# The last tile rows of a mixture-of-experts block: their weighting, adding and norm spread over ScalarE, GpSimd and TensorE

## The chip, the cores and the metric

The kernel runs on one core of a Trainium2 chip, in one launch. Its time is device microseconds of an execution. Three executions of the kernel before took 1188.94, 1193.68 and 1197.59 us, so the median is 1193.68 us. The profile is of a fourth execution, of 1189.59 us, in which the instructions span 1187.8 us.

## The reference

The program computes one transformer block on 512 tokens of width 1024 in f32: a token mixer of two branches, then a mixture of 32 experts of which each token takes two, then a norm. The change touches the end of it alone:

```python
    # hier_moe: each token has two entries (token, expert, weight), sorted by expert
    hid = jax.nn.silu(xblk @ w_gate[e]) * (xblk @ w_up[e])
    yb = hid @ w_down[e]
    y = segment_sum(yb * buf_w[:, None], buf_tok, num_segments=N + 1)[:N]
    ...
    h = h + gt2 * y
    return rmsnorm(h, norm_final_g)
```

`rmsnorm` divides each row of h by the root of its mean square plus 1e-6 and multiplies it with the gain of the final norm.

## The kernel before, in words

**Staging.** The experts are worked in 16 pairs (NPAIR). A pair has 128 rows, 64 for each expert. Per pair, TensorE multiplies the gathered tokens with the gate and up weights (L2638), ScalarE applies the silu (L2189), VectorE the product (L2393), TensorE transposes (L2648) and multiplies with the down weights in two halves of 512 columns (L2661), and VectorE multiplies each half with the gate row of the block into `yo` (`finish`, L2402). Rows of all pairs but the last are stored by GpSimd with an indirect DMA in `y_dram` at the two places of each token (`store`, L2116). The rows of the last pair never go to memory: `matrix(15)` holds, for each of the four tiles of 128 tokens, a 128x128 matrix with the weight of each entry at its token, and TensorE multiplies `yo` with it.

**The four tiles.** The 512 tokens lie in four tiles, i = 0 to 3 (the first to the fourth), and `h[:, i, :]` is tile i, 128x1024 f32. At the end SP loads for each tile two blocks of rows from `y_dram`, j = 0 and 1, 512 KB each (L2071): `ya[2*i]` lies in `uT` and `ya[2*i+1]` in `mg`. Each load has a semaphore `f_in` of its own. `wts[:, j, i]` is a token's weight for its entry j.

**The steps for a tile**, and who does them before the change:
- `summed(i)` (L2438, VectorE, tiles 0 to 2): two instructions of the form h = ya * weight + h, 128x1024 each, with both large inputs in SBUF.
- TensorE's sum (L2737): for tiles 0 to 2 the matrix of the last pair times `yo`. Tile 3 has no `summed`: two diagonal matrices (`diag`, in `wr`) times the loaded rows are added in the same PSUM banks, ahead of the matrix term. It counts `f_c`.
- `whole(i)` (L2482, VectorE): h = h + PSUM. It counts `f_h`.
- ScalarE's square with a sum along the row (L2220), then the root (L2222). The square's output goes to a PSUM bank as `junk`. It counts `f_rt`.
- `normed(i)` (L2486 and L2487, VectorE): reciprocal, then h * reciprocal * gain into `ya[2*i]`, again with two SBUF inputs. It counts `f_o`, and SP stores the tile (L2090).

**What sets the order.** Every engine has a queue written out by hand; an engine stops at each of its waits, and what is queued behind stands still. Chains (`f_link`, `link`) make an engine wait for its own last instruction. `further` (L2005) is a branch that every engine passes just before the end; its body, for tokens beyond the 16 pairs, isn't entered in the profiled execution. ScalarE's functions lie in tables, and a table is loaded by an instruction of its own wherever the one needed may not be there.

Of the kernel before, what the change touches and what calls it, by code (L numbers as in the profile page):

```python
# [150 lines left out]
def build(nc, A, out):  # L151
# [14 lines left out]
    with ExitStack() as top:  # L166
        stage_sems = []

        def sem(name):
            stage_sems.append(nc.alloc_semaphore(name))  # L170
            return stage_sems[-1]
# [1822 lines left out]
        def matrix(b):  # L1994

            return zrT[:, 2 + b % 2, :].rearrange("p (i t) -> p i t", i=NT)
# [1 line left out]
        diag = wr[:, :, :].rearrange("p k n -> p (k n)")[:, 0:2 * P].rearrange("p (j t) -> p j t", j=2)  # L1998
        yo_over = zrT[:, 6:8, :].rearrange("p a n -> p (a n)")
        mat_over = zrT[:, 0, :].rearrange("p (i t) -> p i t", i=NT)  # L2000
        bank_of = (0, 4, 6, 2)

        def two_banks(i):
            return ps[:, bank_of[i]:bank_of[i] + 2, :].rearrange("p b n -> p (b n)")
# [13 lines left out]
        ya = [(uT, mg)[j][:, :, :].rearrange("p a b -> p (a b)")[:, D * i:D * i + D] for i in range(NT) for j in range(2)]  # L2018
        f_in = [sem(f"f_in{n}") for n in range(2 * NT)]
        f_ld, f_warm, f_eps, f_h, f_sq, f_rt, f_o, f_out, f_dve = (sem(f"f_{n}") for n in "ld warm eps h sq rt o out dve".split())  # L2020
        out_t = out[0].rearrange("(i p) d -> i p d", p=P)

        with nc.Block() as block:
            @block.sync
            def _(sp):
# [39 lines left out]
                for q_ in range(2):  # L2065
                    sp.wait_ge(y_st[q_], 16 * (NPAIR // 2 - q_))
                    s_, turns = place_of("g", NPAIR - 1, q_)
                    sp.wait_ge(unit_free[s_], turns + 1 + fills[s_])
                for i in range(NT):
                    for j in range(2):  # L2070
                        sp.dma_start(ya[2 * i + j], y_rows[i, j]).then_inc(f_in[2 * i + j], 16)  # L2071

# [13 lines left out]
                sp.wait_ge(m_h0, 16)  # L2086
                sp.wait_ge(f_ld, 16)
                for i in range(NT):
                    sp.wait_ge(f_o, i + 1)
                    sp.dma_start(out_t[i], ya[2 * i]).then_inc(f_out, 16)  # L2090
                sp.wait_ge(f_out, 16 * NT)

            @block.gpsimd
            def _(pool):
                pool.memset(eps[:, :], 1e-6).then_inc(f_eps, 1)
                pool.wait_ge(m_yTe, NT)
                pool.dma_start(grow2, A["norm_ffn_g"][0].partition_broadcast(P)).then_inc(m_g, 16)
                pool.wait_ge(m_p, 8)
                pool.memset(xg, 0.0).then_inc(x_clear, 1)
                for i in range(NT):  # L2100
                    pool.wait_ge(n2_u, i + 1)
                    pool.dma_start(u2_dram[P * i:P * i + P, :], u2[:, i % 2, :]).then_inc(n2_row, 16)
                    pool.wait_ge(n2_row, 16 * (i + 1))
                pool.wait_ge(m_g, 16)

                def gather(b):
                    q_ = b % 2
                    wait(pool, e_xT, b - 1)
                    pool.indirect_dma_start(xg[:, q_, :], None, u2_dram,
                                            bass.IndirectOffsetOnAxis(ap=slots[:, b:b + 1], axis=0),  # L2110
                                            bounds_check=T - 1, oob_is_err=False)\
                        .then_inc(x_in[q_], 16)

                def store(b):
                    pool.wait_ge(e_y, 2 * b + 2)
                    pool.indirect_dma_start(y_dram, bass.IndirectOffsetOnAxis(ap=y_at[:, b:b + 1], axis=0), yo[:, b % 2, :],  # L2116
                                            None, bounds_check=2 * T - 1, oob_is_err=False)\
                        .then_inc(y_st[b % 2], 16)

                pool.wait_ge(r_sl, 1)  # L2120
                pool.wait_ge(x_clear, 1)
                gather(0)
                gather(1)
                pool.wait_ge(r_ya, 1)
                for b in range(NPAIR):
                    if b + 2 < NPAIR:
                        gather(b + 2)
                    if b < NPAIR - 1:
                        store(b)
                for q_ in range(2):  # L2130
                    pool.wait_ge(y_st[q_], 16 * (NPAIR // 2 - q_))

                def first():
                    pool.wait_ge(e_xT, NPAIR)
                    pool.wait_ge(e_wat, 1)

                def body(v):
                    pool.tensor_copy(idx[:, 0:1], slots[:, bass.ds(v + NPAIR, 1)]).then_inc(v_idx, 1)
                    pool.tensor_copy(ovw[:, 0:1], tok_at[:, bass.ds(v + NPAIR, 1)]).then_inc(v_tok, 1)
                    pool.tensor_copy(ovw[:, 1:2], w_at[:, bass.ds(v + NPAIR, 1)]).then_inc(v_wt, 1)  # L2140
                    pool.wait_ge(v_idx, v + 1)
                    pool.sem_inc(v_seen, 1)
                    pool.indirect_dma_start(xg[:, 0, :], None, u2_dram,
                                            bass.IndirectOffsetOnAxis(ap=idx[:, 0:1], axis=0),
                                            bounds_check=T - 1, oob_is_err=False).then_inc(v_x, 16)
                    pool.wait_ge(v_c, NT * v + NT)
                    pool.sem_inc(v_seen, 1)

                further(pool, first, body)

            @block.scalar
            def _(act):
# [58 lines left out]

                further(act, first, body)

                junk = ps[:, 0:2, :].rearrange("p b n -> p (b n)")
                act.wait_ge(f_warm, 1)
                for i in range(NT):
                    act.wait_ge(f_h, i + 1)
# [8 lines left out]
            def _(dve):  # L2226
# [253 lines left out]
                def whole(i):  # L2480
                    dve.wait_ge(f_c, i + 1)
                    dve.tensor_tensor(h[:, i, :], h[:, i, :], two_banks(i), ALU.add).then_inc(f_h, 1)  # L2482

                def normed(i):
                    dve.wait_ge(f_rt, i + 1)
                    f_link(dve.reciprocal(frt[:, i:i + 1], frt[:, i:i + 1]))  # L2486
                    dve.scalar_tensor_tensor(ya[2 * i], h[:, i, :], frt[:, i:i + 1], gf, ALU.mult, ALU.mult)\  # L2487
                        .then_inc(f_o, 1)

                summed(1)  # L2490
                whole(0)
                summed(2)
                whole(1)
                for i in range(2, NT):
                    normed(i - 2)
                    whole(i)
                normed(NT - 2)
                normed(NT - 1)

            @block.tensor  # L2500
            def _(pe):
# [220 lines left out]
                    pe.wait_ge(v_c, NT * OVER)  # L2722

                further(pe, first, body, last)
                pe.wait_ge(e_y, 2 * NPAIR)
                pe.wait_ge(e_mat, 1)
                for i in range(NT):
                    if i == NT - 1:
                        pe.wait_ge(e_diag, 2)
                        for j in range(2):  # L2730
                            pe.wait_ge(f_in[2 * i + j], 16)
                    for c in range(2):
                        cols = slice(512 * c, 512 * c + 512)
                        terms = [(diag[:, j, :], ya[2 * i + j][:, cols]) for j in range(2)] if i == NT - 1 else []
                        terms.append((matrix(NPAIR - 1)[:, i, :], yo[:, (NPAIR - 1) % 2, cols]))
                        for m, (one, rows) in enumerate(terms):
                            ins = pe.matmul(ps[:, bank_of[i] + c, :], one, rows, start=(m == 0), stop=(m == len(terms) - 1))  # L2737
                    ins.then_inc(f_c, 1)


# [26 lines left out]
```

## Time and profile before

| what | value |
|---|---|
| three executions | 1188.94, 1193.68, 1197.59 us |
| the profiled execution | 1189.59 us |
| its span | 1187.8 us |
| TensorE busy | 1032.5 us (87%) |
| VectorE busy | 418.4 us (35%) |
| ScalarE busy | 204.0 us (17%) |
| GpSimd busy | 150.4 us (13%) |
| last instruction of VectorE ends | 1184.8 us into the span |

The busy shares are means over the whole span. The change touches the last 25 us, where the shares are others: TensorE's last product ends near 1178.7 us, and VectorE is busy nearly without a gap from 1164.4 us on. What that stretch costs is read there, instruction by instruction.

### The profile page before, as it was taken

Reading aid. Unit: us, or ns where it says so; the run is one execution under the profiler, and the core shown is the slowest. Engines: PE = TensorE matmul, PEld = TensorE weight load, DVE = VectorE, ACT = ScalarE, POOL = GpSimd, SP = SyncE. Lnnn points to the kernel's source line nnn. Section 1 sums busy time; section 2 is a strip of 40 time slices with the busy share of each in tenths; the row PEclk is TensorE's granted clock in tenths of the full one; section 3 lists DMA queues with packets and bytes.
Section 4 is the critical chain, followed back from the end, with each engine's and each line's share of the span. In section 5 each row is a group of like instructions: output and inputs, shape, how many; then the busy total and the mean of one; then the engine's idle time right before and its main releaser. Section 6 shows DMA issues by size and latency. Waiting matters only on the chain.

```text
span 1187.8 us, 13390 instructions
## 1 busy us (share of the span) xinstructions
PE 1032.5 (87%) x5421; PEld 503.8 (42%) x5421; DVE 418.4 (35%) x736; ACT 204.0 (17%) x441; POOL 150.4 (13%) x219
## 2 busy tenths in 40 slices
PE   5999999999999898998999668988777788878775
PEld 4443344455445565766455423333333233333332
DVE  4663436563072653457424531111111111110016
ACT  4011123332102564222111100000000000000003
POOL 4100001141200544212000010000000000000000
PEclk9899999999998899999999869999999998998998
DMA  9923427323946001000971569999999999999995
GB/s 351 384 92 106 175 73 283 123 74 148 248 117 163 14 1 37 29 2 2 370 291 52 236 232 431 425 427 427 427 428 426 427 426 428 427 425 428 405 387 216
DMA packets 75760, 301.81 MB, mean 254 GB/s; under 512 B 21478, under 2 KB 27976, under 8 KB 63409
## 3 DMA queue, kind: packets, MB, share of 16 engines
q1 hardware_dynamic: 62178, 280.11, 59.8%
q0 software_dynamic: 6912, 15.59, 3.5%
q10 hardware_dynamic: 6608, 5.24, 1.5%
q8 instruction: 44, 0.72, 0.2%
q14 instruction: 18, 0.15, 0.0%
HBM read 286.03 MB, written 22.03 MB: 259 GB/s over the span
## 4 chain that ended last, share of the span: by engine, by line
PE 25%; DMA 21%; DVE 3%; issue 2%; ACT 1%; DVEq 0%; ACTq 0%; POOLq 0%
PE ps L2638 11%; DMA ring<-in_moe_w_down_dram 9%; DMA ring<-in_moe_w_gate_dram 8%; PE ps L2661 5%; PE ps L2579 5%; PE ps L2530 3%; DMA uT<-in_moe_w_gate_dram 3%; DMA uT<-y_dram 1%; DMA y_dram<-zrT,y_at 1%; PE ps L2546 1%; PE ps L2621 1%; DVE zrT L2385 1%; DVE h L2438 0%; DMA zrT<-u_dram,slots 0%; DVE uT L2487 0%
## 5 line engine op out<-in xcount | busy, mean ns | idle before, releaser
L2638 PE MATMUL ps<-ring,zrT 128*64 128x512 f32 x704 | 204.6, 631 | 40.9 <-issue 17.5
L1047 PE MATMUL ps<-ring,uT 128*128 128x512 f32 x384 | 169.8, 596 | 0.6 <-PE ps L965 0.6
L2638 PEld LDWEIGHTS ps<-ring,zrT 128*64 128x64 f32 x704 | 69.0, 145 | 141.0 <-issue 141.0
L1036 PE MATMUL ps<-uT,ring 128*128 128x512 f32 x256 | 117.3, 615 | 2.0 <-DVE uT L701 1.4
L2402 DVE TENSOR_TENSOR zrT<-ps,mod 128x512 f32<-128x512 f32 x32 | 22.1, 692 | 266.6 <-PE ps L2661 266.3
L1047 PEld LDWEIGHTS ps<-ring,uT 128*128 128x128 f32 x384 | 71.4, 190 | 86.5 <-issue 86.0
L2661 PE MATMUL ps<-ring,hdT 128*64 128x512 f32 x352 | 79.6, 604 | 18.7 <-DMA ring<-in_moe_w_down_dram 16.0
L2189 ACT ACTIVATE zrT<-ps 128x512 f32<-128x512 f32 x16 | 9.6, 597 | 413.4 <-PE ps L2638 413.4
L2638 PE MATMUL ps<-uT,zrT 128*64 128x512 f32 x160 | 72.3, 606 | 6.5 <-issue 6.5
L1036 PEld LDWEIGHTS ps<-uT,ring 128*128 128x128 f32 x256 | 49.4, 197 | 66.7 <-issue 65.4
L2116 POOL DMA_INDIRECT y_dram<-zrT,y_at x15 | 15.2, 1015 | 418.6 <-DVE zrT L2402 418.6
L2393 DVE TENSOR_TENSOR zrT<-zrT,ps 128x512 f32<-128x512 f32 x16 | 11.0, 688 | 143.4 <-PE ps L2638 143.4
L2579 PE MATMUL ps<-ring,uT 128*128 128x512 f32 x128 | 55.8, 593 | 0.0
L2661 PEld LDWEIGHTS ps<-ring,hdT 128*64 128x64 f32 x352 | 29.2, 139 | 61.5 <-issue 61.5
L1123 POOL TENSOR_SCALAR prob<-prob,gate,rsum 128x512 f32<-128x512 f32 (+3 forms) x64 | 40.0, 635 | 103.1 <-DVE rsum L1177 102.2
L2638 PE MATMUL ps<-mg,zrT 128*64 128x512 f32 x80 | 37.0, 617 | 9.8 <-DMA uT<-in_moe_w_gate_dram 6.8
L655 DVE SCALAR_TENSOR_TENSOR acc<-ring,csil,acc 128x512 f32<-128x512 f32 x56 | 43.0, 768 | 2.0
L2661 PE MATMUL ps<-mod,hdT 128*64 128x512 f32 x80 | 36.9, 616 | 7.4 <-DMA mg<-in_moe_w_down_dram 4.9
L2638 PE MATMUL ps<-mod,zrT 128*64 128x512 f32 x80 | 38.6, 639 | 0.0
L1173 DVE TENSOR_REDUCE mx<-ps 128x2 f32<-128x1024 f32 (+3 forms) x32 | 26.4, 824 | 32.5 <-PE ps L1254 32.3
L2661 PE MATMUL ps<-mg,hdT 128*64 128x512 f32 x80 | 37.0, 618 | 0.0
L2579 PEld LDWEIGHTS ps<-ring,uT 128*128 128x128 f32 x128 | 24.0, 190 | 28.7 <-issue 28.7
(428 smaller groups left out, 1296.0 us busy)
## 6 DMA issues: line engine op xcount, KB each, us to landing
ring<-in_moe_w_gate_dram SPq DMA_DIRECT2D x22, 2048.0 KB, 33.0
ring<-in_moe_w_up_dram SPq DMA_DIRECT2D x20, 2048.0 KB, 33.8
ring<-in_moe_w_down_dram SPq DMA_DIRECT2D x18, 2048.0 KB, 33.9
ring<-in_w_in_dram SPq DMA_DIRECT2D x8, 2048.0 KB, 12.5
ring<-in_w_ada_dram SPq DMA_DIRECT2D x8, 2048.0 KB, 8.8
mod<-in_moe_w_down_dram SPq DMA_DIRECT2D x5, 2048.0 KB, 38.3
mg<-in_moe_w_down_dram SPq DMA_DIRECT2D x5, 2048.0 KB, 33.0
uT<-in_moe_w_up_dram SPq DMA_DIRECT2D x5, 2048.0 KB, 37.6
```

Source lines behind the costliest of these rows:

```text
L655: link(dve.scalar_tensor_tensor(a, w[:, k, :], csil[:, k:k + 1], a, ALU.mult, ALU.add))
L1036: ins = pe.matmul(ps[:, n % 4, :], slot(name, KD, w)[:, k, c0:c0 + P], uT[:, k, :], start=(k == 0), stop=(k == KD - 1))
L1047: ins = pe.matmul(ps[:, n % 4, :], uT[:, k, P * i:P * i + P], w, start=(k == 0), stop=(k == KD - 1))
L1123: ins = pool.tensor_scalar(p_, p_, gate[:, i, h3:h3 + 1], rsum[:, t % 4, g:g + 1], ALU.mult, ALU.mult)
L1173: dve.tensor_reduce(mx[:, t % 4, :], ps[:, 2 * (t % 2):2 * (t % 2) + 2, 0:rows_of(t)], AX, ALU.max, negate=True).then_inc(a_mx, 1)
L2116: pool.indirect_dma_start(y_dram, bass.IndirectOffsetOnAxis(ap=y_at[:, b:b + 1], axis=0), yo[:, b % 2, :], None, bounds_check=2 * T - 1, o ...
L2385: dve.tensor_copy(xgT[:, b % 2, :, :], ps[:, 4:6, :].rearrange("p b (k t) -> p (b k) t", k=4))\
L2402: dve.tensor_tensor(yo[:, b % 2, 512 * c:512 * c + 512], ps[:, 2 + c, :], mod[:, 5, 512 * c:512 * c + 512], ALU.mult).then_inc(e_y, 1)
L2530: ins = pe.matmul(ps[:, 2 * (n % 2) + b, :], yT[:, k, P * i:P * i + P], w[:, k, 512 * j:512 * j + 512], start=(k == 0), stop=(k == 3))
L2579: ins = pe.matmul(ps[:, 4 + n % 3, :], mgT[:, k, P * i:P * i + P], slot(f"wo{k // 4}", 4, D)[:, k % 4, 512 * j:512 * j + 512], start=(k == ...
L2638: ins = pe.matmul(ps[HALF * r:HALF * r + HALF, "gu".index(kind), :], xgT[:, b % 2, k, HALF * r:HALF * r + HALF], w[r][:, k, :], start=(k = ...
L2661: ins = pe.matmul(ps[HALF * r:HALF * r + HALF, 2 + c, :], hdT[:, j, HALF * r:HALF * r + HALF], w[r][:, j, 512 * c:512 * c + 512], start=(j ...
```

## The change

Four things are done in other places:
- **Loads.** SP loads the rows of the tiles in the order 3, 0, 2, 1 in place of 0, 1, 2, 3.
- **TensorE.** The diagonal products for tile 3 stand ahead of the waits for the last pair's results, and the matrix products of the four tiles follow. The PSUM banks change with it: tile 3 has banks 0 and 1, tile 0 has 4 and 5, and ScalarE's `junk` is in 4 and 5.
- **Tile 2's rows.** ScalarE multiplies both blocks with the weights, in place. GpSimd adds the two products to h. VectorE waits for GpSimd (`f_p`) ahead of `whole(2)`.
- **Tile 0's norm.** VectorE makes the reciprocal and counts `f_rs`. GpSimd multiplies with the reciprocal and then with the gain, and SP stores tile 0 when GpSimd is done (`f_op`).

VectorE's order is now: `finish` first half, `summed(0)`, `finish` second half, `further`, `summed(1)`, `whole(0)`, `whole(1)`, reciprocal 0, the wait for GpSimd, `whole(2)`, reciprocal 1, `normed(1)`, `whole(3)`, reciprocal 2, `normed(2)`, reciprocal 3, `normed(3)`.

```diff
-        bank_of = (0, 4, 6, 2)
+        bank_of = (4, 6, 2, 0)
...
-                for i in range(NT):
+                for i in (3, 0, 2, 1):
                     for j in range(2):
                         sp.dma_start(ya[2 * i + j], y_rows[i, j]).then_inc(f_in[2 * i + j], 16)
...
                 for i in range(NT):
-                    sp.wait_ge(f_o, i + 1)
+                    if i == 0:
+                        sp.wait_ge(f_op, 1)
+                    else:
+                        sp.wait_ge(f_o, i)
                     sp.dma_start(out_t[i], ya[2 * i]).then_inc(f_out, 16)
...
+                link = Chain(pool, f_pool)
+                for j in range(2):
+                    pool.wait_ge(f_w, j + 1)
+                    link(pool.tensor_tensor(h[:, 2, :], h[:, 2, :], ya[4 + j], ALU.add))
+                pool.sem_inc(f_p, 1)
+                pool.wait_ge(f_ld, 16)
+                pool.wait_ge(f_rs, 1)
+                link(pool.tensor_scalar(ya[0], h[:, 0, :], frt[:, 0:1], None, ALU.mult))
+                pool.tensor_tensor(ya[0], ya[0], gf, ALU.mult).then_inc(f_op, 1)
...
-                junk = ps[:, 0:2, :].rearrange("p b n -> p (b n)")
+                junk = ps[:, 4:6, :].rearrange("p b n -> p (b n)")
+                for j in range(2):
+                    act.wait_ge(f_in[4 + j], 16)
+                    act.activation(ya[4 + j], ya[4 + j], ACT.Copy, scale=wts[:, j, 2:3]).then_inc(f_w, 1)
                 act.wait_ge(f_warm, 1)
...
+                def root_turned(i):
+                    dve.wait_ge(f_rt, i + 1)
+                    dve.reciprocal(frt[:, i:i + 1], frt[:, i:i + 1]).then_inc(f_rs, 1)
+
                 def normed(i):
-                    dve.wait_ge(f_rt, i + 1)
-                    f_link(dve.reciprocal(frt[:, i:i + 1], frt[:, i:i + 1]))
+                    dve.wait_ge(f_rs, i + 1)
                     dve.scalar_tensor_tensor(ya[2 * i], h[:, i, :], frt[:, i:i + 1], gf, ALU.mult, ALU.mult)\
                         .then_inc(f_o, 1)
 
                 summed(1)
                 whole(0)
-                summed(2)
                 whole(1)
-                for i in range(2, NT):
-                    normed(i - 2)
-                    whole(i)
-                normed(NT - 2)
-                normed(NT - 1)
+                root_turned(0)
+                dve.wait_ge(f_p, 1)
+                whole(2)
+                root_turned(1)
+                normed(1)
+                whole(3)
+                for i in (2, 3):
+                    root_turned(i)
+                    normed(i)
...
+                last_tile = NT - 1
+                pe.wait_ge(e_diag, 2)
+                for j in range(2):
+                    pe.wait_ge(f_in[2 * last_tile + j], 16)
+                    for c in range(2):
+                        pe.matmul(ps[:, bank_of[last_tile] + c, :], diag[:, j, :], ya[2 * last_tile + j][:, 512 * c:512 * c + 512],
+                                  start=(j == 0), stop=False)
                 pe.wait_ge(e_y, 2 * NPAIR)
                 pe.wait_ge(e_mat, 1)
```

Two places of the order rest under the prediction. The first is VectorE's queue from the branch to its end. L2438 and L2455 are `summed`, L2482 and L2499 `whole`, L2486 and L2503 the reciprocal, L2487 and L2507 the last step of `normed`. Before:

```order
L2438 SCALAR_TENSOR_TENSOR h<-uT,wts,h 128x1024
L2438 SCALAR_TENSOR_TENSOR h<-mg,wts,h 128x1024
L2482 TENSOR_TENSOR h<-h,ps 128x1024
L2438 SCALAR_TENSOR_TENSOR h<-uT,wts,h 128x1024
L2438 SCALAR_TENSOR_TENSOR h<-mg,wts,h 128x1024
L2482 TENSOR_TENSOR h<-h,ps 128x1024
L2486 RECIPROCAL frt<-frt 128x1
L2487 SCALAR_TENSOR_TENSOR uT<-h,frt,mod 128x1024
L2482 TENSOR_TENSOR h<-h,ps 128x1024
L2486 RECIPROCAL frt<-frt 128x1
```

And of the change:

```order
L2455 SCALAR_TENSOR_TENSOR h<-uT,wts,h 128x1024
L2455 SCALAR_TENSOR_TENSOR h<-mg,wts,h 128x1024
L2499 TENSOR_TENSOR h<-h,ps 128x1024 x2
L2503 RECIPROCAL frt<-frt 128x1
L2499 TENSOR_TENSOR h<-h,ps 128x1024
L2503 RECIPROCAL frt<-frt 128x1
L2507 SCALAR_TENSOR_TENSOR uT<-h,frt,mod 128x1024
```

Two of the `summed` instructions and one of the `normed` are gone from VectorE. They are on GpSimd's queue, behind its branch, as four instructions of which three have two inputs:

```order
L2158 TENSOR_TENSOR h<-h,uT 128x1024
L2158 TENSOR_TENSOR h<-h,mg 128x1024
L2162 TENSOR_SCALAR uT<-h,frt 128x1024
L2163 TENSOR_TENSOR uT<-uT,mod 128x1024
```

GpSimd's queue had nothing behind the branch before. The second place is ScalarE's queue behind its branch, with the waits (the names in brackets are those that the semaphores had when they were first made: a_cT is `f_h`, a_k and a_sc are the `f_in` of tile 2). Before:

```order
L2220 ACT_TABLE_LOAD [waits a_cT]
L2220 ACTIVATE ps,fss<-h 128x1024 [waits a_cex]
L2222 ACT_TABLE_LOAD
L2222 ACTIVATE frt<-fss,eps 128x1 [waits a_cTe]
```

And of the change:

```order
L2231 ACT_TABLE_LOAD
L2231 ACTIVATE uT<-uT,wts 128x1024 [waits a_k]
L2231 ACTIVATE mg<-mg,wts 128x1024 [waits a_sc]
L2237 ACTIVATE ps,fss<-h 128x1024 [waits a_cT,a_cex]
L2239 ACT_TABLE_LOAD
L2239 ACTIVATE frt<-fss,eps 128x1 [waits a_cTe]
```

The table load that waited for the first `whole` now stands ahead of ScalarE's first wait for loaded rows, and the first square has none in front of it. The table load in front of the first root stays.

## Rows read from the trace of the kernel before

**Rows 1.** Chain of waits, last 33 us: start us, us, what:
```profile
1155.61 8.77 DMA uT<-y_dram
...
1164.40 1.28 DVE h L2438
...
1183.48 1.28 DVE uT L2487
```

**Rows 2.** Timeline, VectorE: start us, us, engine line operation, [idle before]:
```profile
1167.32 0.69 DVE L2402 TENSOR_TENSOR zrT<-ps,mod 128x512 f32<-128x512 f32 x1 [0.27 <-DVE h L2438]
1168.57 1.28 DVE L2438 SCALAR_TENSOR_TENSOR h<-uT,wts,h 128x1024 f32<-128x1024 f32 x1 [0.56 <-issue]
1169.89 1.28 DVE L2438 SCALAR_TENSOR_TENSOR h<-mg,wts,h 128x1024 f32<-128x1024 f32 x1
1171.21 1.22 DVE L2482 TENSOR_TENSOR h<-h,ps 128x1024 f32<-128x1024 f32 x1
1176.60 0.16 DVE L2486 RECIPROCAL frt<-frt 128x1 f32<-128x1 f32 x1 [0.40 <-ACT frt L2222]
1178.00 1.21 DVE L2482 TENSOR_TENSOR h<-h,ps 128x1024 f32<-128x1024 f32 x1
```

**Rows 3.** Timeline, ScalarE and TensorE, the end:
```profile
1173.81 1.03 ACT L2220 ACTIVATE ps<-h 128x1024 f32<-128x1024 f32 x1
1174.97 1.28 ACT L2222 ACT_TABLE_LOAD   x1
1176.27 0.29 ACT L2222 ACTIVATE frt<-fss,eps 128x1 f32<-128x1 f32 x1
1163.23 3.65 PE L2661 MATMUL ps<-ring,hdT 128*64 128x512 f32 x16 [1.64 <-DMA ring<-in_moe_w_down_dram]
1168.07 5.42 PE L2737 MATMUL ps<-zrT 128*128 128x512 f32 x12 [1.18 <-DVE zrT L2402]
```

**Rows 4.** Timeline, SP: issue of load 3, 5 and 7 of eight:
```profile
1156.78 0.32 SPq L2071 DMA_DIRECT2D uT<-y_dram  x1
1157.63 0.47 SPq L2071 DMA_DIRECT2D uT<-y_dram  x1
1158.62 0.58 SPq L2071 DMA_DIRECT2D uT<-y_dram  x1
```

**Rows 5.** DMA issues, KB, us to landing: loads 3, 5, 7, 8:
```profile
uT<-y_dram SPq DMA_DIRECT2D x1, 512.0 KB, 10.1
uT<-y_dram SPq DMA_DIRECT2D x1, 512.0 KB, 11.8
uT<-y_dram SPq DMA_DIRECT2D x1, 512.0 KB, 13.3
mg<-y_dram SPq DMA_DIRECT2D x1, 512.0 KB, 13.9
```

**Rows 6.** Timeline, VectorE beside GpSimd, early stage and near 509 us:
```profile
190.69 0.69 DVE L762 TENSOR_TENSOR zrT<-zrT,early 128x512 f32<-128x512 f32 x1
190.95 1.56 POOL L471 TENSOR_TENSOR bt<-lend,early 128x512 f32<-128x512 f32 x1 [4.10 <-DVE zrT L760]
191.42 1.64 DVE L763 TENSOR_TENSOR zrT<-zrT,early 128x512 f32<-128x512 f32 x1
508.88 1.04 POOL L1380 TENSOR_TENSOR yb<-vt,bonus 128x512 f32<-128x512 f32 x1
509.30 1.29 DVE L1481 TENSOR_TENSOR gb<-ps,cst 128x512 f32<-128x512 f32 x2 [4.55 <-PE ps L1626]
```

**Rows 7.** Groups by line: GpSimd's sizes, min/median/max ns or mean ns:
```profile
L468 POOL TENSOR_TENSOR lend<-bt,lend x4: 1258/1268/1740, 185.6 to 244.1; 128x512 f32<-128x512 f32 x4
L499 POOL TENSOR_TENSOR lend<-early,peT x8: 712/718/722, 314.1 to 320.0; 128x248 f32<-128x248 f32 x8
L1123 POOL TENSOR_SCALAR prob<-prob,gate,rsum 128x512 f32<-128x512 f32 x16 | 13.0, 822 | 71.8 <-DVE rsum L1177 71.5
L2172 ACT ACTIVATE zrT<-h 128x1024 f32<-128x1024 f32 x4 | 4.2, 1057 | 0.0
```

More of the change, by code:

```diff
@@ L2020, in build @@
         f_ld, f_warm, f_eps, f_h, f_sq, f_rt, f_o, f_out, f_dve = (sem(f"f_{n}") for n in "ld warm eps h sq rt o out dve".split())
+        f_p, f_pool, f_rs, f_op, f_w = (sem(f"f_{n}") for n in "p pool rs op w".split())
         out_t = out[0].rearrange("(i p) d -> i p d", p=P)
@@ L2727, in _ @@
                 for i in range(NT):
[L2728 to L2731, printed above, removed]
                     for c in range(2):
[L2733 to L2737, printed above, removed]
+                        ins = pe.matmul(ps[:, bank_of[i] + c, :], matrix(NPAIR - 1)[:, i, :],
+                                        yo[:, (NPAIR - 1) % 2, 512 * c:512 * c + 512], start=(i < last_tile), stop=True)
                     ins.then_inc(f_c, 1)
```

## The prediction, made before the changed kernel ran

> **What bounds the kernel now.** I read the chain of waits first, since a mean over the span says nothing of the last 25 us. There TensorE's 87% is no guide: the chain goes from the load of the first returned rows, which lands at 1164.4, through VectorE to its last instruction, which ends at 1184.8 [rows 1]. Store, landing and what lies around them add 4.8 us, to the execution's 1189.59. In the timeline of VectorE the reader is to see the work of the tail, each instruction behind the other: 1.28 us for one step of `summed`, about 1.31 from start to start, 1.22 for a `whole`, then reciprocals and norms [rows 2]. TensorE's products for tiles 0 to 2 start right behind the second half of `finish` and are done long before VectorE asks for them [rows 2, 3]. So the tail is bound by VectorE, and before it by the loads.
>
> The loads come next. SP issues eight within 4 us, but they land one by one: load 3 was issued at 1156.78 and took 10.1 us, so it landed at 1166.9; load 5 at 1157.63 + 11.8 = 1169.4; load 7 at 1158.62 + 13.3 = 1171.9; load 8 about 1.25 later, at 1173.15 [rows 4, 5]. Between them I put load 4 at 1168.2 and load 6 at 1170.7, by the same step. Sizes and issue places stay, so I keep these times and change only whose rows they are.
>
> **The change, part by part.** What leaves VectorE is 2 x 1.31 us (`summed(2)`) and 1.28 us (norm of tile 0), 3.9 us. What it gets for that:
>
> *Load order.* Tile 0 has loads 3 and 4 in place of 1 and 2. `summed(0)` runs 1166.95 to 1168.2 and 1168.3 to 1169.6, and the second half of `finish`, queued behind it, starts near 1169.85, 2.5 us later than its 1167.32 [rows 2]. TensorE fills that time: the last down product ends at 1166.9 [rows 3], and the four diagonal products follow. Six products of this size took 5.42 us in twelve rows [rows 3], 0.86 with the step to the next, so four are 3.4 us and end near 1170.9, against 1170.6 for `finish`. TensorE's gain is nothing, its loss nothing: tile 0's product is ready at about 1172.8, ahead of VectorE. The branch ends about 0.56 us behind `finish` [rows 2], at 1171.1. But tile 1 now has loads 7 and 8: `summed(1)` can start at 1171.95 and, if nothing else is in the way, ends at 1174.5. Before it ended at 1171.2 [rows 2].
>
> *ScalarE's products.* The table load has no wait in front any more and lies in ScalarE's idle time. Load 5 lands at 1169.4; a square of this size from SBUF took 1.06 us [rows 7], and I take the same for the multiplication: the first is ready at 1170.5, the second (load 6) at 1171.8. Nobody else wants ScalarE then, so the cost is nothing.
>
> *GpSimd's adds.* No row has GpSimd at 128x1024. At 512 columns an addition took 1.26 us at its least, at 248 columns 0.72 [rows 7]: 2.05 ns a column, so an estimate of 2.3 us at 1024. The other end is 3.5 us, twice the 1.74 of the slowest. I take 2.3, since the slow rows have a cause, which follows.
>
> *The two engines together.* GpSimd's L471 (two inputs in SBUF) runs from 190.95 to 192.5 [rows 6]. VectorE's L763, also with two inputs in SBUF, starts at 191.42 and takes 1.64 us, while L762, of the same form and size, takes 0.69. 0.95 us too long is what was left of GpSimd's instruction, less the last 0.1. GpSimd's own instruction had been held up by L762. At 509.3 VectorE has one input in PSUM, and two instructions take 1.29 beside GpSimd's, undisturbed. So two such instructions exclude one another, and the form with PSUM is free. `summed` and `normed` are of the first form, `whole` of the second. The Trainium skill says the same (SBUF — State Buffer, section "Who interferes with whom"): a VectorE instruction with two SBUF inputs and a GpSimd instruction that reads SBUF take one port as an exclusive lock, and the later one is blocked until the other is done. By that rule the sum below is +5.3 us, without it +0.8; the trace agrees with the rule.
>
> Now in the tail: GpSimd starts its first addition at about 1170.7 (0.2 us for the hand-over, as behind a root) and holds until 1173.0. The first step of `summed(1)`, due at 1171.95, ends at 1174.15 in place of 1173.2. GpSimd's second addition has been ready since 1173.1 and goes next, 1174.1 to 1176.3. The second step of `summed(1)` ends at 1177.5 in place of 1174.5. **Cost 3.0 us.**
>
> *From there to the end.* `whole(0)` 1177.5 to 1178.7. ScalarE's square, table load and root take 1176.56 - 1173.81 = 2.75 us [rows 3], to 1181.5; `whole(1)` lies beside that. The reciprocal and its hand-over are 0.2 [rows 2]: 1181.7. GpSimd's `f_p` came at 1176.4, so that wait costs nothing; it would from 5.3 us later on. `whole(2)` and all behind it are the same eight instructions as before, which took from 1178.00 to 1184.76 [rows 1, 2], 6.8 us, so they would end at 1188.5. The one table load saved counts only if the chain passes ScalarE; it does now at tile 0, and is in the 2.75.
>
> *GpSimd's norm of tile 0.* It starts at 1181.9. One step with a column of scalars: 0.82 us at 512 columns with two such columns [rows 7], so 1.2 to 1.6 at 1024. Then 2.3 us with two inputs, from 1183.2 to 1185.5. `normed(1)` is due at 1183.2, since the root of tile 1 comes 2.75 - 1.28 = 1.47 us behind the first: a tie. Behind GpSimd it loses 2.2 us; ahead of it, `normed(2)` waits a little and the loss is 0.8. I take 1.5. The store of tile 0 goes out near 1186 and is no longer the last.
>
> **The sum.** Last instruction at 1188.5 + 1.5 = 1190.0 against 1184.8: **+5.3 us**, to 1194.9 by the profiled execution. That one was on the low side: the four executions known have a mean of 1192.4, the three a median of 1193.68. From the first the change comes to 1197.8, from the second to 1199.0; I say **1198**.
>
> **Rivals.**
>
> *A, GpSimd is not in the way (0.17).* If the tie-breaks and the lock cost nothing at this size, `summed(1)` ends at 1174.5, `whole(0)` at 1175.8, the root at 1178.6, `whole(2)` starts at 1178.8 and the end is 1185.6: +0.8 us, 1193. For it: the rows with the lock are of half the size. Against: every VectorE row of this form beside GpSimd's shows it.
>
> *B, the loads come in earlier, and the change is faster (0.06).* VectorE's 3.9 us can be gained only if its rows are there. Were each load in 2.6 us earlier, `finish` would stand at 1167.3, `summed(1)` end at 1171.9, `whole(0)` follow tile 0's product at 1172.6, and `whole(2)` start at 1176.8: end 1183.5, -1.2 us, 1191. It decides from load 4 at 1165.7 and load 8 at 1171.3 on, and it needs case A too. The trace speaks against it: the loads land 1.25 us apart, each behind the other.
>
> *C, GpSimd is slower than I take it (0.12).* At 3.5 us an instruction each of the two adds and the norm's last step hold VectorE 1.1 us longer: +8.6, 1201.
>
> *Forecast (0.65):* +4 to +7, 1196 to 1200 by the middle executions.
>
> **How the numbers follow.** No case moves the time by 1%, which is 12 us and about what a measurement can tell from no change. Single executions of the kernel before spread over 8.7 us, and the median of few of them can lie 3 us off either way; that spread is wider than any case. The range goes from case A and B on a low median, 1190, to case C and the forecast on a high one, 1203. Faster by over 1% would need a median under 1181.7, where no case leads: 0.01. Slower by over 1% needs over 1205.6, case C on a high median: 0.04. Within 1%: 0.95.
>
> **What would show it.** Right: both steps of `summed(1)` over 2.1 us long, the first GpSimd addition begun near 1170.7, tile 1's rows landing last, VectorE idle about 1.6 us ahead of the first reciprocal while ScalarE loads its table, and one `normed` near 3 us beside GpSimd's last instruction. Wrong: steps of `summed(1)` at 1.28 (case A), VectorE waiting for GpSimd ahead of `whole(2)` (case C or worse), `summed(0)` begun before 1165.7 (case B). A stage ahead of 1155 us that differs would be no part of this, since the change leaves it as it is.

## The result

In 20 executions each, the changed kernel has a median of 1196.35 us (1191.75 to 1199.34) and the kernel before 1191.02 us (1188.30 to 1197.59). The ratio is 1.0044, with a 95% interval of 1.0033 to 1.0055: 5.2 us slower, between 3.9 and 6.6. That is slower beyond the measurement's uncertainty and well within 1%. The profiled execution took 1195.72 us, with a span of 1193.9.

Single executions spread over 9.3 us before and 7.6 us now, and a good part of that arises ahead of the place of the change: SP's first load of returned rows goes out anywhere between 1153.7 and 1158.4 us in the profiles below. So this text also counts the **tail**, from the issue of that load to the end of the span, which the trace gives to 0.1 us. Before it is 1187.8 - 1155.6 = 32.2 us [rows 1]; now 1193.9 - 1155.0 = 38.9. All runs that follow are told by it, one profiled execution each.

The tail is good to about half a microsecond. In some of the profiles (before, and five of the runs) SP issues the third load 1.2 us behind the first, and VectorE, which then waits for it in every kernel with tile 3 loaded first, starts 11.3 to 11.5 us behind the first issue; in the others (the change, and six of the runs) it is 1.65 to 1.8 us, and 11.6 to 11.8. Both kinds occur with the same order of loads, so this is not the change's doing. The third load landed 11.3 us behind the first issue before and 11.6 now, so of the 6.7 us it accounts for 0.3.

VectorE in the changed kernel, timeline (start us, us, engine, line, operation, [idle before, and what ended it]):

```profile
1166.64 1.28 DVE L2455 SCALAR_TENSOR_TENSOR h<-uT,wts,h 128x1024 f32<-128x1024 f32 x1 [4.56 <-DMA uT<-y_dram]
1169.55 0.69 DVE L2419 TENSOR_TENSOR zrT<-ps,mod 128x512 f32<-128x512 f32 x1 [0.27 <-DVE h L2455]
1171.74 2.10 DVE L2455 SCALAR_TENSOR_TENSOR h<-uT,wts,h 128x1024 f32<-128x1024 f32 x1 [1.50 <-DMA uT<-y_dram]
1173.87 3.25 DVE L2455 SCALAR_TENSOR_TENSOR h<-mg,wts,h 128x1024 f32<-128x1024 f32 x1
1177.16 2.35 DVE L2499 TENSOR_TENSOR h<-h,ps 128x1024 f32<-128x1024 f32 x2
1181.26 0.17 DVE L2503 RECIPROCAL frt<-frt 128x1 f32<-128x1 f32 x1 [1.76 <-ACT frt L2239]
1181.34 1.22 DVE L2499 TENSOR_TENSOR h<-h,ps 128x1024 f32<-128x1024 f32 x1
1182.83 1.28 DVE L2507 SCALAR_TENSOR_TENSOR uT<-h,frt,mod 128x1024 f32<-128x1024 f32 x1
1185.36 2.61 DVE L2507 SCALAR_TENSOR_TENSOR uT<-h,frt,mod 128x1024 f32<-128x1024 f32 x1
1188.07 1.28 DVE L2507 SCALAR_TENSOR_TENSOR uT<-h,frt,mod 128x1024 f32<-128x1024 f32 x1
```

And GpSimd, with ScalarE's two products and the table load that no longer waits:

```profile
1158.98 1.28 ACT L2231 ACT_TABLE_LOAD   x1
1169.17 1.15 ACT L2231 ACTIVATE uT<-uT,wts 128x1024 f32<-128x1024 f32 x1 [8.91 <-DMA uT<-y_dram]
1170.41 1.15 ACT L2231 ACTIVATE mg<-mg,wts 128x1024 f32<-128x1024 f32 x1
1170.40 2.35 POOL L2158 TENSOR_TENSOR h<-h,uT 128x1024 f32<-128x1024 f32 x1 [21.23 <-ACT uT L2231]
1172.83 3.22 POOL L2158 TENSOR_TENSOR h<-h,mg 128x1024 f32<-128x1024 f32 x1
1181.62 2.84 POOL L2162 TENSOR_SCALAR uT<-h,frt 128x1024 f32<-128x1024 f32 x1 [5.57 <-DVE frt L2503]
1184.54 2.35 POOL L2163 TENSOR_TENSOR uT<-uT,mod 128x1024 f32<-128x1024 f32 x1
```

The reader is to see three VectorE instructions that are too long: 2.10, 3.25 and 2.61 us for a form that took 1.28 each time before [rows 2]. Each overlaps a two-input instruction of GpSimd and ends 1.1 us behind it (1173.84 behind 1172.75, 1177.12 behind 1176.05, 1187.97 behind 1186.89), so nearly all of its 1.28 us of work lies behind GpSimd's end. The second `summed` step (1173.87) started after GpSimd's second addition (1172.83), which itself waited for the first step.

The stores, by the view of DMA issues (KB, us to landing): the first store of the changed kernel and its last one:

```profile
out_dram<-uT SPq DMA_DIRECT2D x1, 512.0 KB, 2.6
out_dram<-uT SPq DMA_DIRECT2D x1, 512.0 KB, 4.1
```

In the kernel before, all four landed in 2.6 us, issued 1.6 to 2.5 us apart. Now SP waits for GpSimd's norm of tile 0 until 1187.0 and then has four stores to issue within 2.4 us.

Split by these instructions, in us from the first load's issue:

| piece | before | after | difference |
|---|---|---|---|
| to the start of `whole(0)` | 15.6 | 22.1 | +6.5 |
| `whole(0)` to `whole(2)`, starts | 6.8 | 4.2 | -2.6 |
| `whole(2)` to the end of the last norm | 6.8 | 8.0 | +1.3 |
| last norm to the end of the span | 3.0 | 4.5 | +1.5 |
| tail | 32.2 | 38.9 | +6.7 |

The tail's 6.7 us lies just above the interval of the ratio, 3.9 to 6.6, and with the 0.3 us taken off just inside it; it is one execution against one.

### The profile page after: what moved, and what is told of

It is laid out like the page before. It is cut to its first block, busy times and chain, and to the rows that moved or that the text cites. A ratio compares the mean times of both kernels' runs of the same rounds, so it can differ in the third digit from the quotient of the medians.

```text
span 1193.9 us, 13395 instructions
## 1 busy us (share of the span) xinstructions
PE 1030.9 (86%) x5421; PEld 504.1 (42%) x5421; DVE 418.6 (35%) x733; ACT 206.5 (17%) x443; POOL 161.2 (14%) x223
## 4 chain that ended last, share of the span: by engine, by line
PE 25%; DMA 22%; DVE 3%; issue 1%; ACT 1%; SPq 0%; ACTq 0%; POOLq 0%; DVEq 0%
DMA uT<-in_moe_w_gate_dram 12%; PE ps L2661 10%; DMA mg<-in_moe_w_down_dram 9%; PE ps L2684 5%; PE ps L2602 5%; PE ps L2553 3%; DMA uT<-y_dram 1%; DMA y_dram<-zrT,y_at 1%; PE ps L2644 1%; DVE zrT L2402 1%; DVE h L2455 0%; DVE uT L2507 0%; DMA zrT<-u_dram,slots 0%; PE ps L2541 0%; PE ps L2569 0%
## 5 line engine op out<-in xcount | busy, mean ns | idle before, releaser
L2661 PE MATMUL ps<-ring,zrT 128*64 128x512 f32 x704 | 201.6, 624 | 38.3 <-issue 16.0
L2419 DVE TENSOR_TENSOR zrT<-ps,mod 128x512 f32<-128x512 f32 x32 | 22.1, 691 | 269.3 <-PE ps L2684 269.1
L1036 PE MATMUL ps<-uT,ring 128*128 128x512 f32 x256 | 114.7, 604 | 2.0 <-DVE uT L701 1.4
L1173 DVE TENSOR_REDUCE mx<-ps 128x2 f32<-128x1024 f32 (+3 forms) x32 | 26.4, 824 | 32.3 <-PE ps L1254 32.1
## 6 DMA issues: line engine op xcount, KB each, us to landing
uT<-in_moe_w_up_dram SPq DMA_DIRECT2D x5, 2048.0 KB, 37.6
```

The source lines that it names most:

```text
L1036: ins = pe.matmul(ps[:, n % 4, :], slot(name, KD, w)[:, k, c0:c0 + P], uT[:, k, :], start=(k == 0), stop=(k == KD - 1))
L1173: dve.tensor_reduce(mx[:, t % 4, :], ps[:, 2 * (t % 2):2 * (t % 2) + 2, 0:rows_of(t)], AX, ALU.max, negate=True).then_inc(a_mx, 1)
L2419: dve.tensor_tensor(yo[:, b % 2, 512 * c:512 * c + 512], ps[:, 2 + c, :], mod[:, 5, 512 * c:512 * c + 512], ALU.mult).then_inc(e_y, 1)
L2661: ins = pe.matmul(ps[HALF * r:HALF * r + HALF, "gu".index(kind), :], xgT[:, b % 2, k, HALF * r:HALF * r + HALF], w[r][:, k, :], start=(k = ...
```

## The experiments

Two theories stood against each other for the first piece: **lock** (a two-input instruction of GpSimd and one of VectorE on SBUF exclude one another) and **loads** (the order of the loads alone). For the last two pieces: the norm on GpSimd, and the queue of stores.

### GpSimd's additions left out

```diff
-                for j in range(2):
-                    pool.wait_ge(f_w, j + 1)
-                    link(pool.tensor_tensor(h[:, 2, :], h[:, 2, :], ya[4 + j], ALU.add))
+                pool.wait_ge(f_w, 2)
```

> The changed kernel without GpSimd's two additions (the second and first block of rows are missing from tile 2; ScalarE's products and all waits stay). Theory lock (an instruction of GpSimd that reads SBUF and one of VectorE with two SBUF inputs exclude one another): both steps of summed(1) take 1.28 us in place of 2.10 and 3.25, whole(0) starts near 1174.5 in place of 1177.2, and everything behind it 2.6 to 2.8 us earlier: span about 1191.2, ratio to before about 1.002. Theory loads (the loss is the order of the loads alone, the long steps are slow rows): the steps stay over 2 us and the time stays at 1.0044.

Measured: ratio 1.0027 (1.0007 to 1.0046), tail 35.9, 2.9 us shorter than the change. VectorE's timeline there:

```profile
1171.99 1.29 DVE L2453 SCALAR_TENSOR_TENSOR h<-uT,wts,h 128x1024 f32<-128x1024 f32 x1 [1.50 <-DMA uT<-y_dram]
1173.31 1.28 DVE L2453 SCALAR_TENSOR_TENSOR h<-mg,wts,h 128x1024 f32<-128x1024 f32 x1
1174.63 2.35 DVE L2497 TENSOR_TENSOR h<-h,ps 128x1024 f32<-128x1024 f32 x2
```

Both steps are back at 1.28, with the same wait for the rows ahead of them. So the additions cause the long steps, at a price of 2.9 us. `whole(0)` starts 19.2 us behind the first issue here, still 3.6 later than before.

### Writing in place of reading

```diff
-                    link(pool.tensor_tensor(h[:, 2, :], h[:, 2, :], ya[4 + j], ALU.add))
+                    for _ in range(2):
+                        link(pool.memset(ya[4 + j], 0.0))
```

> The changed kernel with each of GpSimd's two additions replaced by two fills with zeros of the same 128x1024 block, which only write SBUF, so they run beside both steps of summed(1) (tile 2 lacks its rows). If the lock is on reading, both steps of summed(1) take 1.28 us. If any GpSimd instruction on SBUF locks VectorE out, they take 0.5 to 1 us longer each.

Measured, one execution, timeline:

```profile
1171.19 1.96 POOL L2159 MEMSET uT<- 128x1024 f32 x2 [21.13 <-ACT uT L2232]
1172.54 1.28 DVE L2456 SCALAR_TENSOR_TENSOR h<-uT,wts,h 128x1024 f32<-128x1024 f32 x1 [1.44 <-DMA uT<-y_dram]
1173.20 1.96 POOL L2159 MEMSET mg<- 128x1024 f32 x2
1173.86 1.28 DVE L2456 SCALAR_TENSOR_TENSOR h<-mg,wts,h 128x1024 f32<-128x1024 f32 x1
```

GpSimd is busy on SBUF beside both steps and holds up neither, and the tail is 36.0, that of the run without the additions. It isn't GpSimd's activity, its writing or ScalarE's that costs. What is left is what the additions do and the fills don't: they read, and they read two blocks. Reading alone isn't enough, as the norm's step with a column of scalars shows further down.

### VectorE adds the two products itself

```diff
-                    pool.wait_ge(f_w, j + 1)
-                    link(pool.tensor_tensor(h[:, 2, :], h[:, 2, :], ya[4 + j], ALU.add))
...
+                for j in range(2):
+                    dve.wait_ge(f_w, j + 1)
+                    f_link(dve.tensor_tensor(h[:, 2, :], h[:, 2, :], ya[4 + j], ALU.add))
                 summed(1)
```

> The changed kernel, but VectorE adds ScalarE's two products to tile 2 itself, between the branch and summed(1), while the rows of tile 1 are still landing. Theory lock: VectorE has 1.22 us more twice, 1170.8 to 1173.3, then summed(1) 1173.3 to 1176.0 at 1.28 a step, so whole(0) starts at 1176.0 against 1177.2: 1.1 us faster than the change, ratio about 1.0035. Theory that handing the additions to GpSimd relieves VectorE: 2.4 us slower than the change, ratio about 1.0065.

Measured: ratio 1.0042 (1.0021 to 1.0063), which can't tell 1.0035 from 1.0044. The tail can: 37.5 us, 1.4 shorter than the change, and `whole(0)` starts 20.7 us behind the first issue in place of 22.1. Timeline:

```profile
1170.18 1.23 DVE L2509 TENSOR_TENSOR h<-h,uT 128x1024 f32<-128x1024 f32 x1 [0.55 <-ACT uT L2228]
```

The rival's 2.4 us longer is out. Two additions of 1.23 us on VectorE cost less than having GpSimd do them: 1.5 us against 2.9, both counted at `whole(0)` from the run that has no additions (19.2). They cost VectorE 1.5 and not 2.5 because they begin in the time in which it would have waited for tile 1's rows.

### The order of the loads

Alone, on the kernel before:

```diff
-                for i in range(NT):
+                for i in (3, 0, 2, 1):
```

> The kernel before with one thing changed: the loads in the order 3, 0, 2, 1. Theory loads: tile 0's rows come as loads 3 and 4 and tile 1's as 7 and 8, the second half of finish starts at 1169.7 in place of 1167.3, summed(1) ends near 1174.4 in place of 1171.2, and all behind it stands 3.0 to 3.3 us later: span near 1191, ratio about 1.0027. Rival (VectorE or TensorE have slack that takes it up): under 1 us.

Measured: ratio 1.0021 (1.0003 to 1.0039), tail 35.7, 3.6 us longer than before, and a little more than the expected 3.0 to 3.3. `whole(0)` starts at 19.2 in place of 15.6. That is where it also starts in the changed kernel without the additions, so the first piece's 6.5 us are 3.6 for the loads and 2.9 for the additions: both theories were right about a part.

And in the changed kernel, tile 1 ahead of tile 2:

```diff
-                for i in (3, 0, 2, 1):
+                for i in (3, 0, 1, 2):
```

> The changed kernel with the loads in the order 3, 0, 1, 2, so tile 1 has loads 5 and 6 and tile 2, for ScalarE and GpSimd, 7 and 8. Theory lock: summed(1) runs from 1170.8 to 1173.4 at 1.28 to 1.5 us a step since GpSimd's additions begin at 1172.9 or later; they end near 1177.9, which is about when whole(2) is due, so whole(2) starts near 1178.0 in place of 1181.3: 3 us faster than the change, ratio 1.002. Theory that only the amount of GpSimd's work counts: as the change, 1.0044.

Measured: ratio 1.003 (1.0014 to 1.0045), tail 35.3, 3.6 us shorter than the change. Timeline:

```profile
1169.44 1.28 DVE L2455 SCALAR_TENSOR_TENSOR h<-uT,wts,h 128x1024 f32<-128x1024 f32 x1 [0.56 <-issue]
1170.76 1.28 DVE L2455 SCALAR_TENSOR_TENSOR h<-mg,wts,h 128x1024 f32<-128x1024 f32 x1
1171.53 2.75 POOL L2158 TENSOR_TENSOR h<-h,uT 128x1024 f32<-128x1024 f32 x1 [23.74 <-ACT uT L2231]
1172.08 2.35 DVE L2499 TENSOR_TENSOR h<-h,ps 128x1024 f32<-128x1024 f32 x2
1174.35 2.34 POOL L2158 TENSOR_TENSOR h<-h,mg 128x1024 f32<-128x1024 f32 x1
1176.78 1.22 DVE L2499 TENSOR_TENSOR h<-h,ps 128x1024 f32<-128x1024 f32 x1 [0.43 <-POOLq L2159]
```

The same two additions now lengthen no instruction of VectorE. The first of them has the 0.4 us that it waited for VectorE's second step; the second runs beside the `whole` steps, with PSUM as one input, and neither is longer. They aren't quite free: `whole(2)`, the last line, waits 0.4 us for their result. And not all of the 3.6 us is the lock: tile 1's rows land earlier too, so `summed(1)` starts 4.2 us behind `summed(0)` in place of 5.1.

### The norm of tile 0, and the stores

```diff
-                for i in range(NT):
+                for i in (1, 0, 2, 3):
                     if i == 0:
                         sp.wait_ge(f_op, 1)
```

> The changed kernel with one thing changed: SP waits for and stores tile 1 first, then tile 0, 2, 3. In the change the first store was issued at 1187.0, behind GpSimd's norm, and the last one took 4.1 us to land in place of 2.6. Theory store queue: tile 1 goes out at 1184.2, the last store lands 2.6 to 2.9 us after its issue, span 1.2 to 1.5 us shorter, ratio about 1.0032. Rival (stores beside VectorE's or GpSimd's last work are slower, whatever their order): no change, 4.1 us stays.

Measured: ratio 1.0038 (1.002 to 1.0056), tail 37.6, 1.3 us shorter. Tile 1 goes out 2.7 us ahead of GpSimd's tile 0, and the last store lands in 2.7 us in place of 4.1. So it was the order of the stores that cost the last piece.

```diff
-                pool.wait_ge(f_rs, 1)
-                link(pool.tensor_scalar(ya[0], h[:, 0, :], frt[:, 0:1], None, ALU.mult))
-                pool.tensor_tensor(ya[0], ya[0], gf, ALU.mult).then_inc(f_op, 1)
...
                 root_turned(0)
+                normed(0)
```

> The changed kernel with the norm of tile 0 back on VectorE, right behind the first reciprocal; GpSimd still adds tile 2. Theory lock and store queue: VectorE gets 1.3 us more and loses the 1.3 us by which normed(2) was held up (2.61 in place of 1.28), so its last instruction ends within 0.3 us of 1189.4, the stores go out one by one and the last lands in 2.6 us: span 1.3 us shorter, ratio about 1.0032. Rival (the offload of the norm is worth its 1.3 us): 1.3 us slower, ratio 1.0055.

Measured: ratio 1.0048 (1.0025 to 1.0072), with seven executions no help. In the trace the last norm ends 34.5 us behind the first issue against 34.3, no norm is over 1.28 us, the stores land in 2.6, and the tail is 37.5, 1.4 shorter. Having the norm on GpSimd saved VectorE nothing on balance: `whole(2)` starts 5.5 us behind `whole(0)` here and 4.2 in the change, and the change then loses the 1.3 us again in `normed(2)`. It cost the stores 1.4 us. (This run's first load went out at 1158.4, 3.4 us later than the change's; its longer time is from there.)

### GpSimd's two instructions alone

```diff
                 pool.wait_ge(f_rs, 1)
+                pool.wait_ge(f_o, 3)
```

> The changed kernel with GpSimd's norm of tile 0 held back until VectorE has done its last instruction, to have its two instructions alone. In the change the step with one column of scalars took 2.84 us and the product with the gain 2.35. Theory lock: the first one was held up by normed(1) and takes 1.2 to 1.6 us alone, the second 2.35 as before; normed(2) takes 1.28 in place of 2.61. Rival (that form is slow on GpSimd by itself): 2.8 us again. The span is longer by about 4 us, since the store of tile 0 comes last.

Measured, one execution, timeline:

```profile
1185.71 1.28 DVE L2508 SCALAR_TENSOR_TENSOR uT<-h,frt,mod 128x1024 f32<-128x1024 f32 x1
1187.20 2.84 POOL L2163 TENSOR_SCALAR uT<-h,frt 128x1024 f32<-128x1024 f32 x1 [12.44 <-DVE uT L2508]
1190.13 2.34 POOL L2164 TENSOR_TENSOR uT<-uT,mod 128x1024 f32<-128x1024 f32 x1
```

With VectorE idle the step with one column of scalars still takes 2.84 us. I had it wrong: `normed(1)` didn't hold it up. That form is slow by itself, and it held up nothing either, since in the changed kernel it lies beside `normed(1)`, which took 1.28. `normed(2)` takes 1.28 in place of 2.61, as expected, so it was the product with the gain that held it up. The tail is 45.8 us, 6.9 longer and not 4, since both its instructions now stand behind the last norm and all stores behind them.

The same step in the form of the earlier stage:

```diff
-                link(pool.tensor_scalar(ya[0], h[:, 0, :], frt[:, 0:1], None, ALU.mult))
+                link(pool.tensor_scalar(ya[0], h[:, 0, :], frt[:, 0:1], 1.0, ALU.mult, ALU.mult))
```

> The changed kernel with one thing changed: GpSimd's step with the reciprocal has a second operation, times 1.0 (the form that an earlier stage of the kernel uses with 0.76 us for 512 columns; the form of the change took 2.84 us for 1024, alone as well as beside VectorE). Theory two forms: it takes 1.2 to 1.6 us; the product with the gain then starts near 28.0 us from the first load's issue in place of 29.5, and ends at 30.3 to 31.7, so normed(2) is held up less or normed(1) is held up instead; the last store lands 1 us or more earlier. Rival (1024 columns cost 2.8 in any form): nothing changes.

```profile
1180.84 1.11 POOL L2162 TENSOR_SCALAR uT<-h,frt 128x1024 f32<-128x1024 f32 x1 [5.57 <-DVE frt L2503]
1182.04 2.34 POOL L2163 TENSOR_TENSOR uT<-uT,mod 128x1024 f32<-128x1024 f32 x1
1182.07 3.40 DVE L2507 SCALAR_TENSOR_TENSOR uT<-h,frt,mod 128x1024 f32<-128x1024 f32 x1
```

1.11 us. The product with the gain then began 0.03 us ahead of `normed(1)`, which took 3.40: held up for the whole of it. The tail is 38.2, shorter by 0.7 (0.5 counted from the third load) and not by 1 or more: GpSimd was quicker by 1.7 us, VectorE's last norm ended 0.9 us later, and the stores no longer queued (2.6 us for the last). This is the tie that the prediction had seen, in a kernel in which it comes about.

### TensorE's part undone

```diff
-                last_tile = NT - 1
-                pe.wait_ge(e_diag, 2)
...
+                    if i == NT - 1:
+                        pe.wait_ge(e_diag, 2)
...
```

> The changed kernel with TensorE's part undone: the diagonal products of tile 3 stand behind the products of tiles 0 to 2 again. Counted from the issue of the first load, TensorE then ends near 25.7 us, and VectorE's whole(3) is due at 29.0. Theory (TensorE's part is worth nothing here): every VectorE instruction stays within 0.3 us, the tail stays 38.9 us. Rival (it carries some of what the change gains): the tail is up to 3 us longer.

Measured, one execution: every VectorE instruction within 0.2 us of its place, tail 39.0. TensorE ends at 1183.7 us, 27.4 behind the first issue (I had said 25.7), and `whole(3)` starts at 29.1. Standing ahead of the last results gains nothing here and costs nothing. That holds for the change as it is, in which `whole(3)` comes that late. With tile 1's rows ahead of tile 2's it came at 25.3 us already; an estimate from these two runs is that it would have waited there for nearly 2 us had TensorE's part been undone. That wasn't tried.

### A version drawn from the runs

```diff
-                for i in (3, 0, 2, 1):
+                for i in (0, 3, 1, 2):
...
-                root_turned(0)
+                whole(3)
+                root_turned(0)
+                normed(0)
                 dve.wait_ge(f_p, 1)
                 whole(2)
-                root_turned(1)
-                normed(1)
-                whole(3)
-                for i in (2, 3):
+                for i in (1, 3, 2):
                     root_turned(i)
                     normed(i)
```

> A version drawn from the runs so far: the change with the loads in the order 0, 3, 1, 2 (tile 0 keeps loads 1 and 2, tile 1 has 5 and 6), the tiles worked in the order 0, 1, 3, 2 on TensorE, ScalarE, VectorE and in the stores, all norms on VectorE, and GpSimd only adding tile 2's rows, after summed(1) is over. Counted from the first load's issue: summed(1) from 13.9 to 16.5 undisturbed, GpSimd's additions from 17.6 to 22.4, normed(0) beside the second of them and held up by 0.8 us, whole(2) at 23.4, the last norm at 29.0, against 29.2 before. Theory (VectorE's saved 2.6 us are eaten by the wait for GpSimd): within 0.3 us of the kernel before, ratio 0.9985 to 1.001. Rival (GpSimd's additions cost nothing once they don't overlap summed(1)): 2 us faster than before, ratio 0.998.

Measured: 1189.64 us against 1191.03, ratio 0.999 (0.9974 to 1.0007), tail 32.1 against 32.2. It gives back the 5 us and equals the kernel before; it isn't faster. Timeline:

```profile
1170.20 1.88 PE L2745 MATMUL ps<-mg,wr 128*128 128x512 f32 x4
1171.91 7.03 PE L2751 MATMUL ps<-zrT 128*128 128x512 f32 x16
1172.17 1.28 DVE L2448 SCALAR_TENSOR_TENSOR h<-mg,wts,h 128x1024 f32<-128x1024 f32 x1
1174.50 2.38 POOL L2155 TENSOR_TENSOR h<-h,uT 128x1024 f32<-128x1024 f32 x1 [23.70 <-ACT uT L2224]
1176.96 2.36 POOL L2155 TENSOR_TENSOR h<-h,mg 128x1024 f32<-128x1024 f32 x1
1173.90 1.22 DVE L2492 TENSOR_TENSOR h<-h,ps 128x1024 f32<-128x1024 f32 x1 [0.44 <-PE ps L2751]
1175.55 1.22 DVE L2492 TENSOR_TENSOR h<-h,ps 128x1024 f32<-128x1024 f32 x1 [0.43 <-PE ps L2751]
1177.27 1.22 DVE L2492 TENSOR_TENSOR h<-h,ps 128x1024 f32<-128x1024 f32 x1 [0.49 <-PE ps L2751]
1178.60 1.81 DVE L2500 SCALAR_TENSOR_TENSOR uT<-h,frt,mod 128x1024 f32<-128x1024 f32 x1
1180.33 1.21 DVE L2492 TENSOR_TENSOR h<-h,ps 128x1024 f32<-128x1024 f32 x1
```

`summed(1)` is undisturbed, and `normed(0)` beside the second addition loses 0.5 us. `whole(2)` starts 23.7 us behind the first issue, where before it was 22.4, with `whole(3)` already done. The expectation had the gain eaten by the wait for GpSimd, and the trace doesn't show that: the second addition ended at 1179.32, and `whole(2)` began at 1180.33, right behind `normed(0)`. Three other things ate it. `summed(1)` ended 1.3 us later than before, since its rows are loads 5 and 6 and no longer 3 and 4. Ahead of three `whole` steps VectorE waited for TensorE, 1.4 us in all: the products for the tiles begin at 1171.91, behind the diagonal ones, though `finish` was done at 1169.4. And `normed(0)` lost its 0.5. So in this order of loads TensorE's part, free in the change, is likely to cost something; no run undid it here.

## Why the prediction was right, step by step

The forecast said +5.3 us with the lock as its largest term; the ratio gives +5.2, within 3.9 to 6.6. The time itself was put at 1198 and is 1196.35: the median that it started from, 1193.68 of three executions, is 1191.02 of twenty.

That 5.3 meets 5.2 to a tenth is partly luck. To the end of the last norm the tails give 34.3 - 29.2 = +5.2 us, which is what the forecast's terms add up to (1190.0 - 1184.8). Behind it the forecast had nothing, and the traces have 1.5 us for the stores. Its terms against the trace, by the issue of the first load (1155.6 in the profile that the forecast was made from, 1155.0 in this one):

- **The loads.** Right. The third lands 11.6 us behind the first issue (said: 11.3), the second half of `finish` starts at 14.5 (14.2), `summed(1)` waits for the seventh and starts at 16.7 (16.3). That alone costs 3.6 us, as the kernel before with the new load order shows.
- **ScalarE and GpSimd's sizes.** 1.15 us for a product (1.06), 2.35 for an addition (2.3). The table load went into idle time as read from the order.
- **The lock on `summed(1)`.** Steps of 2.10 and 3.25 us were expected as 2.2 and about 3.3, a cost of 3.0; leaving the additions out gives 2.9. The two rivals to it, slow rows and GpSimd's mere activity, each fell by a run of its own.
- **From `whole(0)` to `whole(2)`.** 4.2 us, as said; this is where 2.6 us come back, of the 3.9 that had left VectorE. Half of the 2.6 is the norm of tile 0, which no longer stands between the first reciprocal and `whole(2)`. The other half lies between `whole(0)` and that reciprocal, 4.1 us in place of 5.4. There VectorE's work wasn't the limit: before, it had 0.4 us of idle time ahead of the reciprocal, waiting for ScalarE's table load, square, table load and root. Had `summed(2)` alone left VectorE, that chain would have kept the 5.4 us (worked out from the rows, no run tried it); the gain needed ScalarE's first table load out of the chain as well. Now VectorE stands idle for 1.8 us there.
- **The norm of tile 0.** The size was near (+1.3 us, said +1.5, between 0.8 and 2.2), the way to it was not. I took 1.2 to 1.6 us for the step with scalars and a tie at `normed(1)`. It takes 2.84, so there was no tie, and the product with the gain held up `normed(2)` instead, 2.61 us long.
- **The stores.** Missed. "The store of tile 0 goes out near 1186 and is no longer the last" is true, and it didn't follow from it that they cost nothing: SP waits for tile 0 first, so tiles 1 to 3 queue behind it, and the last landed in 4.1 us. In the tail this is +1.5 us on top of the forecast. Why the ratio still came to +5.2 and not to 6.7 isn't shown. 0.3 us of it is the issue of the third load; the rest is within the interval. The first piece repeats: in the five runs that leave it alone `whole(0)` starts 21.9 to 22.3 us behind the first issue. The kernel before has one profile only.
- **TensorE's part.** "TensorE's gain is nothing, its loss nothing" holds in the change: undone, nothing moves. In another order of the loads, that of the last version, VectorE's three waits for TensorE speak against it.

Rival A, GpSimd not in the way, fell with the long steps of the changed kernel and with the first experiment. For B, faster by earlier loads, nothing spoke. C, slower GpSimd, was half there in one instruction that it hadn't named.

## What to carry to other kernels

Before work goes from VectorE to GpSimd, look at which VectorE instructions will run beside it: where both read two operands from SBUF they take turns, whole instruction by whole instruction, and work moved away can cost more than work kept (`summed(1)` lost 2.9 us to two additions that cost VectorE 1.5 when it did them itself). In these runs steps with one input in PSUM stood beside GpSimd's additions, and fills beside VectorE's two-input steps, at no cost; the same additions a little later lengthened nothing on VectorE. Look too at what the engine that is relieved waits for next: where that is another engine's chain, the relief turns into idle time. And when a queue takes results in a fixed order, the slowest maker shouldn't stand first in it.

## What the runs showed of the hardware

The form of a GpSimd instruction decides its time and what it gets in the way of. On 128x1024 f32, a product with one column of scalars took 2.84 us in every run that has it, alone or beside VectorE, and with a second operation, times 1.0, 1.11 us. An addition of two blocks took 2.35, a fill 0.95.

The slow form doesn't take turns with VectorE: 2.84 us from 1181.62 and `normed(1)`'s 1.28 from 1182.83 overlap, and neither is longer. The two-input form does, in each case here where VectorE's instruction also had two SBUF inputs. Whether the quick form with scalars does at this size is open: it ran beside a `whole` alone. At 128x512 an early stage of the kernel before shows it taking turns, from 0.76 us to 1.65, behind two instructions of VectorE with two SBUF inputs:

```profile
388.64 1.27 DVE L1156 TENSOR_TENSOR early<-early,cmx 128x512 f32<-128x512 f32 x2
388.82 1.65 POOL L1123 TENSOR_SCALAR prob<-prob,gate,rsum 128x512 f32<-128x512 f32 x1 [0.30 <-DVE rsum L1177]
```

That form reads one block, so GpSimd's instruction needn't have two for this.

The Trainium skill (SBUF — State Buffer, section "Who interferes with whom") has every GpSimd instruction that reads SBUF contend with a two-input VectorE one. The additions agree with it, the fills agree with its exception for writes, and the slow form with one column of scalars doesn't agree; why it is free wasn't tried.
